# A hybrid decoder layer in split float32 on one core: seven gate products in another order, tiles signed and stored a slab later, loads in rings of three, embedding factors made early through HBM

## The reference

```python
u = rms_norm(h, norm_mix_w)
proj = u @ w_in                      # split into 9 parts
o_h = chunk_gated_linear_attention(silu(hq), 1 - f, hi, log(f))    # 8 heads, 128 x 128
o_g = chunk_gated_linear_attention(gq, gk, gv, log_a)              # 4 heads, 128 x 256
y = concat(head_readout(o_h, hz), head_readout(o_g, gz)) @ w_out
h = h + y
e = rms_norm(p @ ple_proj, ple_norm_w)
gate = sigmoid(rms_norm(h, ple_gate_norm_w) @ ple_gate_w + ple_gate_b)
h = h + gate * e
return rms_norm(h, final_norm_w)
```

## Time and profile before

| what | value |
|---|---|
| median of 3 runs | 2294.86 us (2291.0 to 2296.16) |
| the profiled execution's own time | 2292.75 us |
| its span | 2290.7 us |
| TensorE matmul busy | 2169.1 us, 95% |
| VectorE busy | 1505.9 us, 66% |
| ScalarE busy | 995.7 us, 43% |
| moved by DMA | 392.20 MB, mean 171 GB/s |
| mean granted TensorE clock | 0.975 |

### The profile page before, as it was taken

One profiled execution on the slowest core, in us unless ns is written; L12 is line 12 of the kernel. 1 busy time (PEld: TensorE's weight loads), 2 busy tenths in 40 slices (PEclk: granted clock), 3 DMA queues, 4 the chain that ended last, 5 costly groups with the idle time before them and its releaser, 6 DMA issues.

```text
span 2290.7 us, 30047 instructions
## 1 busy us (share of the span) xinstructions
PE 2169.1 (95%) x10202; PEld 1805.3 (79%) x10202; DVE 1505.9 (66%) x2976; ACT 995.7 (43%) x1742; POOL 161.2 (7%) x244
## 2 busy tenths in 40 slices
PE   9999999999999999999999999998999886899883
PEld 8888888888888888888888888887787765678663
DVE  8577777766657767766765655575576564456877
ACT  7444454444334544444443433353543443333433
POOL 1001111000000000101010100001100002000000
PEclk9999999999999999999999999999999898899996
DMA  9436656565446543536364743356766668744545
GB/s 335 151 118 175 177 152 177 162 170 154 127 127 170 149 135 108 158 117 176 99 183 166 218 139 110 101 144 197 274 222 212 229 202 248 230 166 147 184 165 175
DMA packets 126905, 392.20 MB, mean 171 GB/s; under 512 B 14816, under 2 KB 20320, under 8 KB 125280
## 3 DMA queue, kind: packets, MB, share of 16 engines
q1 hardware_dynamic: 106720, 279.89, 35.7%
q0 software_dynamic: 20096, 111.16, 19.4%
HBM read 349.05 MB, written 142.61 MB: 215 GB/s over the span
## 4 chain that ended last, share of the span: by engine, by line
PE 72%; DVE 12%; DMA 10%; ACT 3%; issue 2%; SPq 1%; DVEq 0%; ACTq 0%
PE acc L897 20%; PE acc L899 20%; PE acc L898 20%; DVE w_lo L1720 4%; PE lv L990 3%; DMA glr_r<-h_kept 3%; DMA h_kept<-feat 3%; DMA w_raw<-in_slabs 2%; DMA h_kept<-work 2%; PE so L999 1%; PE so L1002 1%; PE so L979 1%; ACT w_hi L1216 1%; DVE work L2284 1%; DMA glr_all<-h_kept 1%
## 5 line engine op out<-in xcount | busy, mean ns | idle before, releaser
L897 PE MATMUL acc<-act_hi,w_lo 128*128 128x512 f32 x2376 | 963.4, 405 | 46.9 <-ACT w_hi L1216 18.5
L899 PE MATMUL acc<-act_hi,w_hi 128*128 128x512 f32 x2376 | 931.9, 392 | 0.0
L898 PE MATMUL acc<-act_lo,w_hi 128*128 128x512 f32 x2376 | 931.6, 392 | 0.0
L897 PEld LDWEIGHTS acc<-act_hi,w_lo 128*128 128x128 f32 x2376 | 451.6, 190 | 142.2 <-issue 50.1
L1216 ACT CAST w_hi<-w_raw 128x1024 fp32r<-128x1024 f32 x339 | 343.0, 1048 | 457.3 <-PE acc L899 337.9
L899 PEld LDWEIGHTS acc<-act_hi,w_hi 128*128 128x128 f32 x2376 | 449.7, 189 | 96.5
L898 PEld LDWEIGHTS acc<-act_lo,w_hi 128*128 128x128 f32 x2376 | 451.6, 190 | 85.3 <-issue 1.5
L1720 DVE TENSOR_TENSOR w_lo<-w_raw,w_hi 128x1024 fp32r<-128x1024 f32 x339 | 402.5, 1221 | 157.2 <-ACT w_hi L1216 153.5
L1289 ACT ACTIVATE work<-work 128x512 f32<-128x512 f32 x120 | 75.8, 632 | 147.8 <-DVE work L1776 147.2
L897 PE MATMUL tr<-act_hi,w_lo 128*128 128x512 f32 x192 | 80.7, 420 | 39.5 <-DVE w_lo L1720 39.5
L1790 DVE COPY_PREDICATED work<-mask_sb,lv 128x256 f32<-128x256 uint8 x168 | 88.8, 529 | 7.4
(11 more groups left out here) (358 smaller groups left out, 2467.0 us busy)
## 6 DMA issues: line engine op xcount, KB each, us to landing
w_raw<-in_slabs SPq DMA_DIRECT2D x276, 512.0 KB, 4.4
w_sums<-in_slabs POOLq DMA_DIRECT2D x96, 512.0 KB, 6.1
w_raw<-w_sums SPq DMA_DIRECT2D x64, 512.0 KB, 3.5
w_sums<-w_sums POOLq DMA_DIRECT2D x32, 512.0 KB, 4.0
work<-e_scratch SPq DMA_DIRECT2D x56, 256.0 KB, 4.8
t_sums<-y_scratch POOLq DMA_DIRECT2D x24, 512.0 KB, 6.2
t_sums<-h_signed POOLq DMA_DIRECT2D x24, 512.0 KB, 9.5
feat<-in_x_feat SPq DMA_DIRECT2D x8, 1024.0 KB, 12.2
```

The lines of the kernel that those rows point to most:

```text
L897: nc.tensor.matmul(ps, lhs_lo, rhs_hi, start=start, stop=False)
L898: nc.tensor.matmul(ps, lhs_hi, rhs_lo, start=False, stop=False)
L899: return nc.tensor.matmul(ps, lhs_hi, rhs_hi, start=False, stop=stop)
```

## The change

1. `GATE_PARTS` runs P5, P6, P7, P4, P3 instead of P6, P7, P5, P4, P3. The first block sum that is needed is then G1 instead of G2. P5 is copied out of PSUM by ScalarE (`part_copy`), P6 and P7 are two VectorE operations per tile each (P6 had one, P7 one, P5 two). The tiles of some blocks stand in the other buffer (`gate_at`).
2. `sign_tile` of slab `n - 2` in pass `n`, right behind the weights; `store_signed` of slab `n - 3`; six semaphores `h_out` instead of four.
3. `load_tile` has three buffers each, waits for the sum of tile `q - 3`, and loads the second tile of slab `n` and the first of slab `n + 1` in SP's pass `n`. The sigmoid is written in place.
4. In slabs 8 to 14 VectorE makes the embedding factors of 21 tiles (`early_embed`, tiles 8 to 28), three per slab; SP loads them from `e_scratch` (`load_early`), stores them to a new HBM tensor `e_ready` (`store_early`), and `load_tile` reads them from there.
5. The row factor of half 0 is made in slab 25 instead of 27, and the 16 `f_scale` operations stand in slabs 25 (2), 26 (3) and 27 (11) instead of at the end.

```diff
-GATE_GROUPS = (21, 22, 20, 23, 24)
+GATE_GROUPS = (20, 21, 22, 23, 24)
-              + [(what, i) for what in (P6, P7, P5, P4, P3) for i in range(4)])
+              + [(what, i) for what in (P5, P6, P7, P4, P3) for i in range(4)])
...
-        e_in = [unit(16), unit(19)]
+        e_in = [unit(16), unit(19), unit(18)]
-        h_in = [glr_r[:, :].bitcast(F32), None]
+        h_in = [glr_r[:, :].bitcast(F32), None, unit(20)]
+        early = [[unit(17), unit(20), unit(21)], e_in]
...
+        EARLY_AT = {n: range(HK + 3 * (n - 8), HK + 3 * (n - 8) + 3) for n in range(8, 15)}
+        MADE_EARLY = range(HK, HK + 3 * len(EARLY_AT))
...
             def load_tile(q):
-                if q >= 2:
-                    sp.wait_ge(g2_sum, q - 1)
-                sp.dma_start(e_in[q % 2], e_scratch[h * KT + c]).then_inc(e_loaded[q % 2], 16)
-                sp.dma_start(h_in[q % 2], h_kept[h, c]).then_inc(e_loaded[q % 2], 16)
+                if q >= 3:
+                    sp.wait_ge(g2_sum, q - 2)
+                if q == HK:
+                    for i in range(2):
+                        sp.wait_ge(early_stored[i], HALVES * KT // 4 * 16 + (4 - i) * 3 * 16)
+                sp.dma_start(e_in[q % 3], e_ready[q] if q in MADE_EARLY else e_scratch[h * KT + c]).then_inc(e_loaded[q % 3], 16)
+                sp.dma_start(h_in[q % 3], h_kept[h, c]).then_inc(e_loaded[q % 3], 16)
+
+            def load_early(n):
+                turn = n // 2 - 4
+                if n == 8:
+                    sp.wait_ge(g2_ready, HK)
+                if turn:
+                    sp.wait_ge(early_stored[n % 2], HALVES * KT // 4 * 16 + turn * 3 * 16)
+                for i in range(3):
+                    h, c = G_TILES[EARLY_AT[n][i]][0:2]
+                    sp.dma_start(early[n % 2][i], e_scratch[h * KT + c]).then_inc(early_loaded[n % 2], 16)
+
+            def store_early(n):
+                for i in range(3):
+                    q = EARLY_AT[n][i]
+                    sp.wait_ge(early_made, q - HK + 1)
+                    sp.dma_start(e_ready[q], early[n % 2][i]).then_inc(early_stored[n % 2], 16)
...
-                    if (n - 2, j) in ENDS_AT:
-                        store_signed(ENDS_AT[n - 2, j])
+                    if (n - 3, j) in ENDS_AT:
+                        store_signed(ENDS_AT[n - 3, j])
...
             for n in range(4, OUT_SLABS):
                 split_weights(S_OUT + n + 1, (n + 1) % 2)
+                for j in range(2):
+                    if (n - 2, j) in ENDS_AT:
+                        sign_tile(n - 2, j)
...
             def g_embed(q):
+                if q not in MADE_EARLY:
+                    st.mark(v.scalar_tensor_tensor(out=e_in[q % 3], in0=e_in[q % 3], scalar=g_vec[:, 3 * c + 1:3 * c + 2], in1=r_e[h],
+                                                   op0=ALU.mult, op1=ALU.mult))
...
+            SCALES_AT = {25: range(0, 2), 26: range(2, 5), 27: range(5, KT)}
...
-            for u in range(0, 6):
-                f_scale(u)
             z_variance(0)
             z_factor(0)
             z_variance(1)
             z_factor(1)
-            for u in range(6, KT):
-                f_scale(u)
```

More of the change, by code:

```diff
@@ L204, in fresh, with build @@
             self.n = 0
-def build(nc, x_feat, p, slabs, w_glr, w2, vec, lb_rows, masks, restart, ident_d, out, e_scratch, y_scratch, w_sums, t_sums, h_kept, h_signed):
+def build(nc, x_feat, p, slabs, w_glr, w2, vec, lb_rows, masks, restart, ident_d, out, e_scratch, y_scratch, w_sums, t_sums, h_kept, h_signed, e_ready):
     with ExitStack() as ctx:
@@ L682, in store_out @@
                 sp.wait_ge(f_scaled, h * KT + (n + 1))
-                sp.dma_start(out[h, n], (feat, work)[h][:, n, :]).then_inc(out_stored, 16)
+                sp.dma_start(out[h, n], gate_at(h, n)).then_inc(out_stored, 16)
             load_slab(S_OUT + 1)
@@ L716, in _ @@
                 if n == 0:
-                    for q in (30, 31):
-                        keep_h(q)
-                    for q in (28, 29, 30, 31):
-                        store_signed(q)
-                for j in range(2):
-                    if (n, j) in G_NO:
-                        load_tile(G_NO[n, j])
+                    keep_h(30)
+                    keep_h(31)
+                if n < 3:
+                    store_signed(26 + 2 * n)
+                    store_signed(27 + 2 * n)
+                if n - 1 in EARLY_AT:
+                    store_early(n - 1)
+                if (n, 1) in G_NO:
+                    load_tile(G_NO[n, 1])
+                if (n + 1, 0) in G_NO:
+                    load_tile(G_NO[n + 1, 0])
                 if n + 1 < GATE_SLABS:
@@ L726, in _ @@
                         load_gate_t(a, k)
+                if n == 8:
+                    load_early(n)
+                if n + 1 in EARLY_AT and n >= 8:
+                    load_early(n + 1)
                 if n == 4:
@@ L2257, in g_part @@
-                if what == P2:
-                    vec_e.wait_ge(*tile_stored(c))
-                    vec_e.wait_ge(*p1_copied(c))
-                    v.tensor_tensor(tile(h, ct), ps, feat[:, HK + c, :], ALU.add).then_inc(free, 1)
-                    return
-                vec_e.wait_ge(out_free[gate_place(n - 4, j)], gate_freed(n - 4))
-                if what == P5:
-                    vec_e.wait_ge(*tile_stored(HK + c))
+                    vec_e.wait_ge(free, gate_freed(n))
+                    st.mark(v.tensor_tensor(feat[:, HK + c, :], work[:, c, :], work[:, HK + c, :], ALU.subtract))
+                elif what == P7:
+                    st.wait()
@@ L2269, in g_part @@
                 else:
-                    v.tensor_tensor(work[:, c, :], work[:, c, :], ps, ALU.add).then_inc(free, 1)
+                    v.tensor_tensor(feat[:, HK + c, :], ps, feat[:, HK + c, :], ALU.subtract).then_inc(free, 1)
             def g_logits(n, j):
@@ L2330, in _ @@
                     g_sum_up(G_NO[n, 0])
+                if n in EARLY_AT:
+                    early_embed(n)
+                for u in SCALES_AT.get(n, ()):
+                    if u == 9:
+                        g_add(G_NO[n, 0])
+                    f_scale(u)
                 if n < GATE_SLABS - 1:
@@ L2335, in _ @@
                         g_embed(G_NO[n, 1])
[L2336 removed]
+                if (n, 0) in G_NO and n < GATE_SLABS - 1:
                     g_add(G_NO[n, 0])
@@ L2467 @@
     h_signed = nc.dram_tensor("h_signed", (HALVES, KT, P, TH), F32, kind="Internal").ap()
-    build(nc, *aps, out, e_scratch, y_scratch, w_sums, t_sums, h_kept, h_signed)
+    e_ready = nc.dram_tensor("e_ready", (E_TILES, P, TH), F32, kind="Internal").ap()
+    build(nc, *aps, out, e_scratch, y_scratch, w_sums, t_sums, h_kept, h_signed, e_ready)
     r = run_bass_kernel_spmd(nc, [{f"in_{k}": v for k, v in arrays.items()}], core_ids=[0])
```

146 lines of the change are left out of this document (78 added, 68 removed).

## The result

| | median us | runs | ratio to before |
|---|---|---|---|
| before | 2295.51 (2291.0 to 2300.26) | 4 | |
| changed | 2220.41 (2217.17 to 2222.99) | 4 | 0.9672 [0.9647, 0.9697] |

The change is faster by 3.3%, 75 us. The forecast was 2199 us with a range from 2160 to 2240: right in direction and inside the range, and the gain was set 20 us too large. The profiled execution took 2218.32 us, its span is 2216.5, so against the 2292.75 of the profile before it is 74.4 us, where the sum said 93.9.

What follows compares the result with a forecast made beforehand. TensorE's pace of 10.88 us per slab bounds the kernel, with 126.4 us of stalls from waits ahead of weights, and VectorE in late gate slabs. 2292.75 - (39.5 + 27.4 + 25.5 + 1.5) gave 2199 us, range 2160 to 2240.

Steps and rivals of the forecast that it cites:

- Output stage: Output slabs: sign_tile one slab later covers the landing of h_kept; 5 us of 44.4 us stall stay, gain 39.5 us.
- Rival 3: Output stage: the wait for h_kept goes from ScalarE to SP, half the gain is kept, 2218 us; chance 0.09.
- Gate slabs 0 to 15: These slabs: of 49.4 us of stall, 22 us stay because of DMA work, gain 27.4 us.
- work of 183 us at a share of at most 0.93 needs 197 us: Gate slabs 0 to 15: DMA work needs 197 us where 16 slabs at pace need 174.1, leaving 22 us of stall.
- Rival 2: Gate stage: DMA is the bound at 256 GB/s, the 49.4 us stay but for 1.4, 2225 us; chance 0.17.
- The 11 MB: Gate slabs 0 to 15: 21 added loads and 21 stores of 256 KB, priced at 33 us of DMA work.
- The reasons given for that gain: Gate slabs 0 to 15: earlier sum of G1 and a third tile buffer mostly end the reasons for 49.4 us of stall.
- Gate slabs 16 to 27: These slabs: VectorE's passes get shorter without tile waits and factor; stall 7 us instead of 32.6, gain 25.5 us.
- VectorE's lag over TensorE starts at 2.9 us: Late gate slabs: the lag grows from 2.9 us to about 9.5 at slab 23, where 0.4 us are lost.
- Three per slab, 2.2 us, cost nothing while the loads come: Gate slabs 8 to 14: VectorE's 21 early factor operations of 0.75 us fit in its free time at no cost.
- Rival 4: Gate stage: early factors' store and load landings hold up queued weights, seven slabs lose 85 us, 2311 us; chance 0.03.
- The end: After TensorE's last matmul: last part starts 4.7 us later, 6.1 us saved behind it, gain 1.5 us.

Runs made afterwards that it cites:

- no_early_factors: The changed kernel with each embedding factor made in its tile's own pass, as before the change, without early loads and stores; 2212.74 us, ratio 0.9663.
- g3_sums_later: The changed kernel with GpSimd adding G3 only after the fills of G1 are made, G4's copies and adds moving too; 2213.79 us, ratio 0.9672.
- five_fill_buffers: The changed kernel without early factors, with five buffers instead of three for tiles read back and split, two taken from tile loads; 2214.27 us, ratio 0.9663.

## Why the prediction was right, and where its size was off

- **Output stage: -39.5 forecast, -39.7 measured** (44.5 to 4.8). Moving the wait by one slab hid the landings of `h_kept`, 3.2 to 9.2 us each in this stage, with the clock and the share as worked out. The two experiments that do and undo this part show it. Rival 3, that SP would take over the wait, fell: SP waited for an older `h_signed` once, 5.3 us.
- **Gate slabs 0 to 15: -27.4 forecast, -17.3 measured.** The step that failed is "work of 183 us at a share of at most 0.93 needs 197 us". The work was even less, 138.28 x 0.86 + 67.92 x 0.80 = 173 us. But the step spread it over 16 slabs, as if it could slide. It can't: the adds of G2 and G3 are issued together at 1886, G1 is read back beside them, and that makes one gap of 19.3 us at a share of 1.02 to 1.05; the stretch from slab 10 on then has room, with 0.80. The loss stands in slabs 7 to 9 (28.5 of 32.1 us), where the prediction's signs had put it (slabs 5 to 9, share above 0.9). Rival 2 named DMA as the bound but kept it over the whole stage, at 48 us of loss, which is not what is seen. The 11 MB, on which the 22 us rested, had no part in that gap; leaving them out left it at 26 us.
- **The reasons given for that gain.** "G1, whose sum GpSimd ends two steps earlier" and "the third buffer" did not bring it: delaying G1's loads to where G2 is done, and taking the third buffer away, each cost nothing that can be told. 13.7 us of the 17.3 came with part 2, most of it in gate slabs 0 and 1, whose 11.9 us the prediction had counted among the stalls that G1 and the third buffer would end. That the sum came within 10 us here is luck.
- **Gate slabs 16 to 27: -25.5 forecast, -12.6 measured** (32.7 to 20.1). The lengths of the passes were right within about 0.1 us in slabs 17, 21 and 24 (12.72 and 11.40; slab 24 was 10.21, worked out as 10.1; slab 25 was 16.54, worked out as 10.1 + 4.66 + 2 x 0.67 = 16.1, so 0.4 short). The term that failed is the start: "VectorE's lag over TensorE starts at 2.9 us". In `no_early_factors` the low weights start 2.3 us into slab 16, in the changed kernel 5.3, and there the wait for the last early stores then adds 5.71 us in one pass. So the lag was at its limit at slab 17 and not at 23: slabs 16 to 24 lose 10.6 us instead of 0.4. The growth was also counted too low: from 2.9 us, four P7 slabs at 1.7 give 9.7 at the end of slab 19, where the prediction has 9.5 only at slab 23; by its own terms 1.5 to 2 us would have been lost there. Slabs 25 to 27 lose 9.5 where about 6.6 were set. Which part of the change brought the 12.6 us is argued only: neither the third buffer nor the ready factors, by the two runs without them, which leaves the earlier place of the loads.
- **"Three per slab, 2.2 us, cost nothing while the loads come"**: the loads did not come. The prediction said that VectorE waiting for early loads would show the forecast wrong, and it waited 5 times. Rival 4 had the mechanism, the circle of store, landing, load and landing with the weights behind it, but priced it with landings of 19 us; the stores landed in 4.6 to 9.4 us, under the 16.4 from which it would have turned the sign. Neither the forecast nor the rival saw that the loads for slab 16 stand behind the last store's landing.
- **The end: -1.5 forecast, -5.4 measured.** The last part started 11.2 us after the last matmul, not 14, and lasted 25.7 instead of 26.8.

Together: 39.7 + 17.3 + 12.6 + 5.4 = 75.0 us, which is the difference of the spans, 74.2, plus 0.7 us that the output stage started later.

**The rate of the DMA engines.** The prediction weighed a limit of about 358 GB/s of HBM for one core (the Trainium skill, DMA: Bandwidth & Descriptors, Specifications) against the rows. The trace speaks against pricing this mix by it: in the gap the engines were full, share 1.02, at 234 GB/s. But the rate is not out of reach: in `g3_sums_later` a window of 20 us shows 360 GB/s at a share of 1.02. These rates count a transfer once, also one from HBM to HBM: over the changed kernel's run the profile has 182 GB/s moved, and 227 GB/s of reads and writes of HBM. So they don't test the limit itself. The Trainium skill, on the same page (Queues, rings and completion order), says that each DMA engine takes turns between the queues for which it has work. What the trace shows agrees as far as it goes: beside GpSimd's burst SP's first three loads of G1 went on, at 17 to 28 us each, where the medians of the same lines over the changed kernel's run are 5.6 to 7.5, and the first of them, issued behind all eight adds, landed at 1907.88, ahead of the last add at 1915.04; no run here shows the turns themselves.

## What to carry to other kernels

A wait that stands in front of the next slab's work on an in-order engine is worth moving by one slab before anything else: it cost no instruction here and brought more than half of the gain. A budget of transfers must be drawn up for the slabs in which they are issued together, not for the stage, and of two producers of traffic each can seem to cost some 5 us or less when it alone is taken away or moved, where both together are worth 17 to 20. And a trip through memory that takes work from a busy stretch must be free in the stretch where it is done, down to the wait for its last store: here that wait made the engine late just before the work it was to relieve.

## What the runs showed of the hardware that was not expected

The rate at a full DMA share is not one number: 234 GB/s in the 24 us from 1886.40 on, in which the accumulating transfers between HBM tensors of G2 and G3 ran; 313 GB/s in the 25 us behind, with the last of them, the copies and adds of G4, and more of SP's loads; 360 GB/s in a window of 20 us of `g3_sums_later`. A plain load of 256 KB took 25.22 us beside that burst in `five_fill_buffers` and 28.4 us in `no_early_factors`.
